# Down bias carried by the first scatter, permuted reads of the gate and up sums, and the turning of gathered rows ahead of the down matmuls

## What is computed

```python
logits = tok @ w_router + b_router
top_val, top_idx = lax.top_k(logits, 4)              # 32 experts
top_w = jax.nn.softmax(top_val, axis=-1)
# for each expert e, on the rows that chose it:
gu = xe @ w_gate_up[e] + b_gate_up[e]                # 1024 -> 2048
g = jnp.minimum(gu[:, 0::2], 7)
u = jnp.clip(gu[:, 1::2], -7, 7)
act = (u + 1.0) * (g * jax.nn.sigmoid(1.702 * g))
y = act @ w_down[e] + b_down[e]                      # 1024 -> 1024
# out[token] += top_w * y ;  x = x + out
```

## Time and profile before

| | |
|---|---|
| median of 3 runs | 1418.37 us (1415.72 to 1419.71) |
| the profiled execution | 1419.66 us, its span 1417.5 us |
| PE busy | 1312.0 us (93%) |
| PEld, DVE, ACT, POOL busy | 533.6, 357.3, 271.1, 34.8 us |
| mean granted TensorE clock | 0.954 of full speed |
| DMA | 470.19 MB, mean 332 GB/s |
| expert units issued at L2047 | 192, of 2,048 KB each |

### The profile page before, as it was taken

One profiled execution on the slowest core, in us unless ns is written; L12 is line 12 of the kernel. 1 busy time (PEld: TensorE's weight loads), 2 busy tenths in 40 slices (PEclk: granted clock), 3 DMA queues, 4 the chain that ended last, 5 costly groups with the idle time before them and its releaser, 6 DMA issues.

```text
span 1417.5 us, 15625 instructions
## 1 busy us (share of the span) xinstructions
PE 1312.0 (93%) x6345; PEld 533.6 (38%) x6345; DVE 357.3 (25%) x604; ACT 271.1 (19%) x520; POOL 34.8 (2%) x43
## 2 busy tenths in 40 slices
PE   6997788899777999999999999999999999999998
PEld 3466544444534233333333333333333333333332
DVE  1237560032405222113121131212212222112122
ACT  2116223310322011111111111111111111111111
POOL 0011230000000000000000000000000000000000
PEclk9999859999997799999999999999999999999999
DMA  9242028875027299999999999999999999999995
GB/s 340 103 168 78 0 61 318 313 271 206 12 96 320 90 386 429 429 429 428 428 429 428 429 429 429 428 428 429 429 429 429 429 428 428 429 428 429 429 429 223
DMA packets 54621, 470.19 MB, mean 332 GB/s; under 512 B 6417, under 2 KB 6673, under 8 KB 27972
## 3 DMA queue, kind: packets, MB, share of 16 engines
q1 hardware_dynamic: 52852, 463.69, 78.9%
q0 software_dynamic: 1744, 6.14, 1.4%
HBM read 463.94 MB, written 5.88 MB: 331 GB/s over the span
## 4 chain that ended last, share of the span: by engine, by line
PE 87%; DVE 5%; ACT 5%; DMA 2%; issue 1%; ACTq 0%; SPq 0%; DVEq 0%
PE PS L929 30%; PE PS L960 16%; PE PS L888 6%; PE PS L909 5%; PE PS L365 4%; PE PS L665 3%; PE PS L392 2%; PE PS L707 2%; PE PS L840 2%; DMA ring<-in_w_gate_up 2%; PE PS L897 1%; PE PS L625 1%; PE PS L950 1%; ACT arena L1848 1%; PE PS L719 1%
## 5 line engine op out<-in xcount | busy, mean ns | idle before, releaser
L929 PE MATMUL PS<-ring,arena 128*64 128x512 f32 x1792 | 400.4, 595 | 1.2 <-ACT arena L1832 0.8
L960 PE MATMUL PS<-ring,arena 128*64 128x512 f32 x1024 | 240.6, 613 | 21.6 <-ACT arena L1848 21.6
L929 PEld LDWEIGHTS PS<-ring,arena 128*64 128x64 f32 x1792 | 129.0, 138 | 258.7 <-issue 257.2
L960 PEld LDWEIGHTS PS<-ring,arena 128*64 128x64 f32 x1024 | 69.4, 139 | 149.5 <-issue 120.2
L1529 DVE TENSOR_SCALAR arena<-PS 128x512 f32<-128x512 f32 x32 | 22.1, 692 | 393.7 <-PE PS L929 393.7
L1482 DVE TENSOR_TENSOR X<-X,PS 128x1024 f32<-128x1024 f32 x34 | 41.5, 1221 | 292.6 <-PE PS L909 292.6
L1845 ACT ACTIVATE arena<-arena 128x512 f32<-128x512 f32 x32 | 20.1, 629 | 477.3 <-DVE arena L1529 477.3
L888 PE MATMUL PS<-arena 128*64 128x512 f32 (+1 forms) x396 | 98.1, 613 | 0.0
L909 PE MATMUL PS<-arena 128*64 128x512 f32 x340 | 81.3, 592 | 1.4 <-ACT arena L1855 1.4
L840 PE MATMUL PS<-arena 32*64 32x512 f32 x264 | 63.2, 614 | 0.0
L365 PE MATMUL PS<-ring,arena 128*128 128x512 f32 x128 | 58.2, 619 | 0.0
(11 more groups left out here) (329 smaller groups left out, 1053.4 us busy)
## 6 DMA issues: line engine op xcount, KB each, us to landing
ring<-in_w_gate_up SPq DMA_DIRECT2D x112, 2048.0 KB, 18.2
ring<-in_w_down SPq DMA_DIRECT2D x64, 2048.0 KB, 15.8
arena<-in_w_gate_up SPq DMA_DIRECT2D x16, 2048.0 KB, 21.3
ring<-in_w_in SPq DMA_DIRECT2D x6, 2048.0 KB, 17.5
ring<-in_cache_win_k SPq DMA_DIRECT2D x8, 1024.0 KB, 6.9
ring<-in_cache_win_v SPq DMA_DIRECT2D x8, 1024.0 KB, 10.6
ring<-in_w_out SPq DMA_DIRECT2D x2, 2048.0 KB, 13.7
ring<-in_cache_mem_k SPq DMA_DIRECT2D x4, 1024.0 KB, 7.5
```

What stands on the lines that cost most here:

```text
L929: last = mm(PS[64 * half:64 * half + 64, nb, :], XT[:, k, :], w[:, k % 2, c:c + 512], start=False, stop=k == KT - 1, tile_position=(0, 64 ...
L960: last = mm(PS[64 * half:64 * half + 64, 5, :], AT[:, k % 4, 64 * (k // 4):64 * (k // 4) + 64], w[:, k % 4, half * 512:(half + 1) * 512], ...
```

## The change

1. The down biases are loaded into the first 32 rows of YB (BD goes), and ScalarE copies the turned GW into the first 32 rows of SW (GWT goes). VectorE clears only rows 32 to 127 of YB, in two instructions, and SW in one. The first scatter, which multiplied zeros, now adds the bias. L872 and the additions L1495 and L1499 go, with the counts of the semaphores behind them.
2. The gate and up biases stand in rows 32 to 95 instead of 0 to 63, and EROW is written on all partitions.
3. G1 and U1 are read from PSUM in the permuted order (innermost step of eight floats instead of two) and written straight, so that L1534 reads and writes straight.
4. `turn_gathered` stands behind the turning of the activation, before the down matmuls; ScalarE's copy to XT stands before its copy of the scatter weights.

```diff
-        BD = ar(7424, D)
-        GWT = ar(9472, NTOK)
-        DOWN_BIAS_BANKS = ((4, 5), (6, 7), (3, 3))
...
-                        r = slice(NE * nb, NE * nb + NE)
+                        r = slice(NE * (nb + 1), NE * (nb + 2))
...
-            pe.wait_ge(sem("logit_parts_kept"), 2)
-            for t in range(3):
-                n = ROWS[t]
-                if t == 1:
-                    pe.wait_ge(sem("scatter_added"), 1)
-                for half in range(2):
-                    r = slice(0, n) if t < 2 else slice(n * half, n * half + n)
-                    last = mm(PS[r, DOWN_BIAS_BANKS[t][half], :], GWT[0:NE, COL0[t]:COL0[t] + n],
-                              BD[0:NE, half * 512:(half + 1) * 512], start=True, stop=True)
-                last.then_inc(sem("scattered"), 1)
...
                 last.then_inc(sem("act_turned"), 1)
+                turn_gathered(q + 1)
 
                 pe.wait_ge(sem("at_ready"), it + 1)
...
                             turned.then_inc(sem("sw_turned"), 1)
-                        turn_gathered(q + 1)
                 last.then_inc(sem("down_ready"), 1)
...
-            v.memset(YB, 0.0).then_inc(sem("y_rows_ready"), 1)
-            v.memset(SW[:, 0:P], 0.0).then_inc(sem("sw_ready"), 1)
-            v.memset(SW[:, P:3 * P], 0.0).then_inc(sem("sw_cleared"), 1)
+            v.memset(YB[NE:2 * NE], 0.0)
+            v.memset(YB[2 * NE:4 * NE], 0.0).then_inc(sem("y_rows_ready"), 1)
+            v.memset(SW, 0.0).then_inc(sem("sw_cleared"), 1)
...
-            for t in range(3):
-                n = ROWS[t]
-                b = DOWN_BIAS_BANKS[t][0]
-                dve.wait_ge(sem("scattered"), t + 1)
-                if t < 2:
-                    x = X[0:n, t, :].rearrange("p (b c) -> p b c", b=2)
-                    ins = v.tensor_tensor(x, x, PS[0:n, b:b + 2, :], ALU.add)
-                else:
-                    for half in range(2):
-                        x = X[0:n, t, half * 512:(half + 1) * 512]
-                        ins = v.tensor_tensor(x, PS[n * half:n * half + n, b, :], x, ALU.add)
-                ins.then_inc(sem("scatter_added"), 1)
-            dve.wait_ge(sem("scatter_added"), 4)
...
-                        gu = PS[:, 0:2, :].rearrange("p b (c two) -> p b c two", two=2)
-                        v.tensor_scalar(G1, gu[:, :, :, 0], 7.0, None, ALU.min).then_inc(sem("gate_ready"), 1)
-                        v.tensor_scalar(U1, gu[:, :, :, 1], 7.0, -7.0, ALU.min, ALU.max).then_inc(sem("expert_steps"), 1)
+                        gu = PS[:, 0:2, :].rearrange("q b (p c two) -> q two c b p", c=4, two=2)
+                        by_part = dict(c=4, b=2)
+                        v.tensor_scalar(G1.rearrange("q (c b p) -> q c b p", **by_part), gu[:, 0], 7.0, None, ALU.min).then_inc(sem("gate_ready"), 1)
+                        v.tensor_scalar(U1.rearrange("q (c b p) -> q c b p", **by_part), gu[:, 1], 7.0, -7.0, ALU.min, ALU.max).then_inc(sem("expert_steps"), 1)
...
-                        v.scalar_tensor_tensor(AC.rearrange("q (c p) -> q p c", c=4),
-                                               U1.rearrange("q b c -> q (b c)").rearrange("q (p c) -> q p c", c=4), 1.0,
-                                               SG.rearrange("q b c -> q (b c)").rearrange("q (p c) -> q p c", c=4),
-                                               ALU.add, ALU.mult).then_inc(sem("act_ready"), 1)
+                        v.scalar_tensor_tensor(AC, U1, 1.0, SG, ALU.add, ALU.mult).then_inc(sem("act_ready"), 1)
...
-            s.copy(GWT[0:NE], PS[0:NE, 3, 0:NTOK]).then_inc(sem("logit_parts_kept"), 1)
+            act.wait_ge(sem("sw_cleared"), 1)
+            s.copy(SW[0:NE, 0:NTOK], PS[0:NE, 3, 0:NTOK]).then_inc(sem("sw_ready"), 1)
...
                         s.copy(AT, PS[:, 4, :].rearrange("p (c n) -> p c n", c=4)).then_inc(sem("at_ready"), 1)
+                        keep_columns(q + 1)
                         if odd:
...
-                        keep_columns(q + 1)
...
-            pool.dma_start(BD[0:NE], a["b_down"].rearrange("l e f -> (l e) f")
+            pool.dma_start(YB[0:NE], a["b_down"].rearrange("l e (h c) -> (l e) h c", h=2)
```

More of the change, by code:

```diff
@@ L286, in build @@
         SELW = ar(10464, 3, 2, SLOTS)
-        G1 = ar(10848, 2, SLOTS * 4)
-        SG = ar(11360, 2, SLOTS * 4)
-        U1 = ar(11872, 2, SLOTS * 4)
+        G1 = ar(10848, 512)
+        SG = ar(11360, 512)
+        U1 = ar(11872, 512)
         AC = ar(12384, 512)
@@ L838, in gate_up_biases @@
                     for nb in range(2):
-                        r = slice(NE * nb, NE * nb + NE)
+                        r = slice(NE * (nb + 1), NE * (nb + 2))
                         last = mm(PS[64 * half:64 * half + 64, nb, :], EROW[r, :], BGU[r, half * 512:(half + 1) * 512],
-                                  start=True, stop=False, tile_position=(NE * nb, 64 * half))
+                                  start=True, stop=False, tile_position=(NE * (nb + 1), 64 * half))
                 last.then_inc(sem("bias_added"), 1)
@@ L902, in scatter @@
                 if banks == (6, 7):
-                    pe.wait_ge(sem("scatter_added"), n + 4)
+                    pe.wait_ge(sem("scatter_added"), n + 1)
                 for half in range(2):
@@ L1410, in expert_row @@
             def expert_row(e):
-                v.tensor_scalar(EROW[0:2 * NE, :], cst("ones")[0:2 * NE, 0:SLOTS], cst("expert")[0:2 * NE, bass.ds(e, 1)], None,
+                v.tensor_scalar(EROW[:, :], cst("ones")[:, 0:SLOTS], cst("expert")[:, bass.ds(e, 1)], None,
                                 ALU.mult).then_inc(sem("erow_ready"), 1)
             keep_columns(6)
-            v.memset(YB, 0.0).then_inc(sem("y_rows_ready"), 1)
-            v.memset(SW[:, 0:P], 0.0).then_inc(sem("sw_ready"), 1)
-            v.memset(SW[:, P:3 * P], 0.0).then_inc(sem("sw_cleared"), 1)
+            v.memset(YB[NE:2 * NE], 0.0)
+            v.memset(YB[2 * NE:4 * NE], 0.0).then_inc(sem("y_rows_ready"), 1)
+            v.memset(SW, 0.0).then_inc(sem("sw_cleared"), 1)
             v.memset(AC, 0.0).then_inc(sem("act_ready"), 1)
@@ L1515, in add_rows @@
                         def add_rows(t):
-                            dve.wait_ge(sem("scattered"), 3 * group + t + 4)
+                            dve.wait_ge(sem("scattered"), 3 * group + t + 1)
                             add_scattered(t, 6)
@@ L1549, in _ @@
                 for t in range(3):
-                    dve.wait_ge(sem("scattered"), last + t + 4)
+                    dve.wait_ge(sem("scattered"), last + t + 1)
                     add_scattered(t, LAST_BANKS[t][0])
@@ L1555, in _ @@
                 dve.wait_ge(sem("slots_moved"), r + 1)
-                dve.wait_ge(sem("scatter_added"), last + 7)
+                dve.wait_ge(sem("scatter_added"), last + 4)
                 v.memset(SW, 0.0).then_inc(sem("sw_cleared"), 1)
@@ L1950, in _ @@
             for nb in range(2):
-                pool.dma_start(BGU[NE * nb:NE * nb + NE].rearrange("p (h c) -> p h c", h=2),
+                pool.dma_start(BGU[NE * (nb + 1):NE * (nb + 2)].rearrange("p (h c) -> p h c", h=2),
                                a["b_gate_up"].rearrange("l e (h b c) -> b (l e) h c", h=2, b=2)[nb]
                                ).then_inc(sem("expert_biases_loaded"), 16)
-            pool.dma_start(BD[0:NE], a["b_down"].rearrange("l e f -> (l e) f")
+            pool.dma_start(YB[0:NE], a["b_down"].rearrange("l e (h c) -> (l e) h c", h=2)
                            ).then_inc(sem("expert_biases_loaded"), 16)
@@ L2097, in _ @@
                 dst = o["y_prompt"][0, t * P:(t + 1) * P] if t < 2 else o["y_sample"].rearrange("b t d -> (b t) d")
-                sp.wait_ge(sem("scatter_added"), npass * (3 * (NE // 2 + 1)) + t + 2)
+                sp.wait_ge(sem("scatter_added"), npass * (3 * (NE // 2 + 1)) + max(t - 1, 0))
                 sp.dma_start(dst, X[0:n, t, :]).then_inc(sem("rows_stored"), 16)
```

## The result

The changed kernel takes 1408.5 us (median of 10 runs, 1402.39 to 1409.51), the kernel before 1415.4 us (median of 10, 1411.93 to 1420.41). The ratio is 0.9944, with a 95% interval of 0.993 to 0.9958: 0.56% faster, which is 7.9 us of 1415.4, with 5.9 to 9.9 us by the interval. The two medians lie 6.9 us apart. Forecast were 8.2 us. One execution of the kernel before, among the 27 that stand beside e1 to e4, took 2007.94 us at a mean granted clock of 0.636, and the ratios leave it out.

The account below looks back on a forecast made before the run. The stream of expert weights was taken as the bound. Stream start 7.2, gaps 0.4, last expert's down matmuls 0.54 and product 0.1 gave 8.2 us: 1410.2 us from the median, range 1406 to 1415 us.

Parts of the forecast that it names:

- The bound: Expert stage: the DMA stream of expert weights at 429 GB/s sets the end, TensorE only slightly faster; chance 0.76.
- the rival: Experts: TensorE sets the end, its 21.6 us saved counting in full, 1389 us; shares chance 0.05 with an earlier clock rise.
- Part 1: Before the experts: down bias moved into the first scatter, L872 gone, stream starts 7.2 us earlier; bounds 6.6 and 9.0 us.
- The cleared rows: Before the experts: VectorE clears accumulator rows in two pieces, 0.9 us more, covered by its 1.7 us wait for the logits.
- The clock: Expert 0: full clock returns 4.1 us after dense work starts, first issue 479.5 us; rival, only at 480 us, chance 0.08.
- Part 2: Gathered rows turned ahead of the down matmuls: TensorE gains 21.6 us in all, mainly the last expert's 0.54 us counting.
- The gaps of the stream: First expert: unit 5 and the next expert's unit 0 issued some 0.9 us earlier, worth 0.4 us; bounds 0 and 2 us.
- The waits for DMA: Experts: TensorE's matmuls wait longer for weights, some 20 us in all, at no cost to the total.
- Part 3: Permuted gate and up reads: straight product saves VectorE 0.37 us, reads cost 0 to 0.76 us; net per expert taken as 0.
- that price: G1 and U1 reads of PSUM: if each new line cost, 0.39 us added in the last expert, sum 7.9 us.
- The product's term: Last expert: the straight product L1534 saves VectorE 0.37 us, of which TensorE takes at most 0.1 us.
- I take 0 for them: Gate and up biases on rows 32 to 95: each product keeps its shape, so the shift is worth 0 us.

Follow-up runs that it names:

- e1: Changed kernel with turned rows back between the down matmuls and reads in order, keeping down bias and shifted bias rows: 1408.43 us, ratio 0.9951.
- e4: Changed kernel with the first output store waiting for its own tile's addition, not the next tile's: 1407.36 us, ratio 0.993 to the kernel before.
- e7: Changed kernel with the gathered rows' transposes done four times in each expert, to load TensorE: 1408.05 us, ratio 0.9945 to the kernel before.
- e6: Changed kernel with the gathered rows' transposes done twice in each expert, to load TensorE: 1407.32 us, ratio 0.9936 to the kernel before.
- e5: Kernel before with the gathered rows' transposes done twice in each expert, to load TensorE: 1423.36 us, ratio 1.0058 to the kernel before.
- e9: Changed kernel timed again, unchanged, on the chip of the two idle-product runs: 1406.33 us, ratio 0.9926 to the kernel before.
- e2: Kernel before with only the turning of the gathered rows moved ahead of the down matmuls: 1414.83 us, ratio 0.9993 to the kernel before.
- e8: Changed kernel with the gate and up biases back on rows 0 to 63: 1407.93 us, ratio 0.9948 to the kernel before.
- e3: Kernel before with only the permuted reads of gate and up: 1416.75 us, ratio 1.001 to the kernel before.
- e11: Changed kernel with the store wait mended and seven idle TensorE products, five of them of 512 columns: 1403.35 us, ratio 0.9917 to the kernel before.
- e10: Changed kernel with the store wait mended and seven idle TensorE products of 256 columns: 1402.56 us, ratio 0.9908 to the kernel before.

## Why the prediction was right

**The bound.** Right, and the experiments leave no room for the rival: e1 and e7, and less sharply e6, rule TensorE out as what sets the changed kernel's end, and e5 shows that in the kernel before it stood within a microsecond or two of doing so: of the 8.7 us that the load was worth there, about 8 showed. That the two bounds met was the reading that mattered: of 21.6 us taken from TensorE almost nothing was to be had.

**Part 1.** 7.2 us forecast; 9.4 - 2.2 = 7.2 us measured, and in e1 too. What made this exact was to ask what stood hidden behind the removed matmuls: TensorE's read of npass. All of L872 would have been 9.0 us. The cleared rows cost nothing, as said (9.55 us from the logits' product to the selection against 9.56), but they used more of the cover than the 0.9 us forecast: VectorE's wait for the logits fell from 1.65 to 0.27 us.

**The clock.** It did come back behind the dense work: expert 0 began at 466.35 us and the grant is 0.99 from 470 to 480 us. In this execution it had been up for part of the gather already (0.67 from 460 to 470 us), which gives 1.4 us of the 10.2; e9, the same kernel, has 19.3 us for the stretch, so this is no effect of the change.

**Part 2.** 0.54 us in the last expert: 4.78 before, 1392.52 - 1388.32 = 4.20 us now, so 0.58. The gaps of the stream: 0.4 us forecast, 0.5 in these two profiles. The four profiles without part 2 have 913.4 to 913.7 us from first issue to last landing, the nine with it 912.1 to 913.4 us, so a gain of under a microsecond is likely, and its size isn't shown. The waits for DMA were forecast as some 20 us from a row of PEld, which counts more than TensorE's own; in the rows of PE they went from 0.3 to 37.8 us, and 21.8 us where only part 2 was made (e2). The other 16 us come with the shifted bias rows (e8).

**Part 3.** The reads cost nothing, as taken. One float of each 8 bytes or of each 32 is the same 692 ns. The Trainium skill, "SBUF — State Buffer", section "Door 1: The DMA port swizzle", tells of a penalty for each new line in SBUF, and of PSUM that a pattern that isn't contiguous slows matmuls. The forecast set that price beside VectorE's reads of PSUM; it doesn't show in them at all, whichever the step. (With it, the forecast's own terms give 7.2 + 0.4 + 0.54 - 0.39 = 7.75 us, not 7.9.) The product's term was mis-sized: 0.1 us forecast, 0.60 us measured, because the shift of the bias rows, which I took at 0, shortens TensorE's side of the same wait. The product alone brings nothing (e3), the rows alone 0.25 us (e1 against before), both 0.60 us. That was the step that failed: "I take 0 for them".

**What was missed.** The first store's wait costs 1.3 us (e4). It stands in the change's SyncE line (`t + 2` became `max(t - 1, 0)`), and the forecast doesn't speak of it. The two errors, 0.5 us too little and 1.3 us too much, leave landing to end at 17.2 us, 0.7 us above forecast. The sum by the corrected terms is 7.2 + 0.58 + 0.60 - 1.3 + about 0.4 = 7.5 us, and the ratio gives 7.9 us with 5.9 to 9.9. That 8.2 lies so near 7.9 is in part luck, since the two errors pull opposite ways and the interval is 4 us wide; that the bound and part 1 were right is not.

## What to carry to other kernels

An engine that is busy for 93% and fills the chain may still not be the bound: compare the last landing with the first issue plus bytes by rate, and look whether issue to landing grows. If it does, the engine is running ahead of the stream, and only an earlier start of the stream or a shorter way behind its last landing counts. Look then for what stands idle before the stream starts, and price a removed step by what was hidden behind it, every wait count that changes with it included.

## What was not expected of the hardware

Here four passes of 32 rows started together with a pair of the gather's on rows 0 to 31 when they were on rows 32 to 95, and only two when they were on rows 0 to 63: 264 passes were busy for 36.8 us in place of 63.2 us, with no other edit (e8).

Idle products in TensorE's waits raised the granted clock ahead of the work that needs it: 0.97 in place of 0.50 from 450 to 460 us, and 12 passes of the gather in 2.97 us in place of 5.0 (e11). The timed runs' mean granted clock is 0.966 in e11 and 0.963 in e10 against 0.960 in e9.

The stretch ahead of the experts ended anywhere from 450.8 to 459.3 us in thirteen profiles, while the 913 us of the stream varied by 1.6 us: this points to its front as the source of most of the spread in this kernel's times.
